# Two experts of each mixture in fixed places, and the loop of spare blocks moved behind the static blocks

## The reference

```python
pg = softmax(xt @ w_group + b_group)                    # 4 groups, the best one is taken
g_prob, g_idx = lax.top_k(pg, 1)
le = (xt @ w_expert + b_expert).reshape(N, 4, 8)[arange(N), g_idx[:, 0]]
e_prob, e_local = lax.top_k(softmax(le), 2)             # 2 of the 8 experts of that group
...
def expert_block(args):
    xb, e = args                                        # up to 128 rows of one expert
    return (silu(xb @ w_gate[e]) * (xb @ w_up[e])) @ w_down[e]
```

## Time and profile before

| | |
|---|---|
| median of 3 runs | 3689.51 us (3687.7 to 3690.94) |
| the profiled execution, its own time | 3681.5 us |
| its span in the trace | 3679.7 us |
| PE busy | 3420.4 us, 93% |
| DVE, ACT, POOL busy | 1617.9, 818.3, 364.8 us |
| m0 | 676 to 1233 us of the span |
| m1 | 1991 to 2548 us |
| m2 | 3300 to 3627 us |
| read from HBM | 752.52 MB, 227 GB/s over the span |

### The profile page before, as it was taken

The page is one execution under the profiler, slowest core; times in us unless marked ns, Lnnn a source line. Parts: engine busy times, 40 slices in busy tenths (PEclk is TensorE's granted clock), DMA queues, the critical chain, the costliest instruction groups (busy, mean ns, idle before and its releaser), DMA issues. The chain is left out here.

```text
span 3679.7 us, 51768 instructions
## 1 busy us (share of the span) xinstructions
PE 3420.4 (93%) x20970; PEld 1738.1 (47%) x20970; DVE 1617.9 (44%) x2560; ACT 818.3 (22%) x1822; POOL 364.8 (10%) x355
## 2 busy tenths in 40 slices
PE   9999999899999899999998998998899978997996
PEld 4444665433333344777754333333455658553332
DVE  4750886510111475777756111113341875462114
ACT  0000650100000122555511000000233551111112
POOL 0010300210000000000000200000000820003110
PEclk9999999899999999999999999999999999999998
DMA  9990211599999621000023999997421402219996
GB/s 373 361 336 0 93 70 69 227 416 427 423 424 424 251 91 57 26 1 1 1 92 142 403 425 425 426 421 303 149 82 68 149 18 79 101 66 371 419 418 267
DMA packets 146694, 818.42 MB, mean 222 GB/s; under 512 B 29875, under 2 KB 35635, under 8 KB 100374
## 3 DMA queue, kind: packets, MB, share of 16 engines
q1 hardware_dynamic: 117910, 737.21, 50.1%
q0 software_dynamic: 25808, 68.88, 4.9%
q10 hardware_dynamic: 2736, 8.95, 0.6%
HBM read 752.52 MB, written 82.55 MB: 227 GB/s over the span
## 5 line engine op out<-in xcount | busy, mean ns | idle before, releaser
L2320 PE MATMUL m_yp<-m_w,m_hidT 128*32 128x512 f32 (+2 forms) x2248 | 378.9, 596 | 10.5 <-issue 4.6
L2297 PE MATMUL m_up<-m_w,m_xT 128*32 128x512 f32 (+2 forms) x1792 | 305.4, 608 | 20.3 <-DMA m_w<-in_moe_w_up 20.3
L2297 PE MATMUL m_gp<-m_w,m_xT 128*32 128x512 f32 (+2 forms) x1792 | 300.7, 598 | 9.8 <-DMA m_w<-in_moe_w_gate 5.4
L2078 DVE TENSOR_TENSOR m_hid<-m_sg,m_up 128x512 f32<-128x512 f32 x42 | 28.9, 688 | 573.9 <-PE m_up L2297 573.9
L2073 DVE TENSOR_TENSOR m_yt<-m_yp,keep_flat 128x512 f32<-128x512 f32 x128 | 82.5, 686 | 398.7 <-PE m_yp L2320 388.9
L2320 PEld LDWEIGHTS m_yp<-m_w,m_hidT 128*32 128x32 f32 (+2 forms) x2248 | 121.7, 124 | 219.6 <-issue 214.1
L2378 ACT ACTIVATE m_sg<-m_gp 128x512 f32<-128x512 f32 (+1 forms) x64 | 33.5, 524 | 786.1 <-PE m_gp L2297 539.2
L2297 PEld LDWEIGHTS m_up<-m_w,m_xT 128*32 128x32 f32 (+2 forms) x1792 | 104.2, 126 | 216.0 <-issue 216.0
L2297 PEld LDWEIGHTS m_gp<-m_w,m_xT 128*32 128x32 f32 (+2 forms) x1792 | 97.5, 124 | 206.7 <-issue 204.1
L434 PE MATMUL front_acc<-front_hT,front_wt 128*128 128x512 f32 x448 | 194.4, 594 | 0.4 <-DVE q0T L535 0.4
L1233 PE MATMUL n_acc<-n_wt,n_hT 128*128 128x512 f32 (+2 forms) x512 | 190.5, 528 | 2.0 <-DMA n_wt<-in_w_in 1.3
(11 more groups left out here) (505 smaller groups left out, 5032.8 us busy)
## 6 DMA issues: line engine op xcount, KB each, us to landing
m_w<-in_moe_w_gate SPq DMA_DIRECT2D x64, 2048.0 KB
m_w<-in_moe_w_up SPq DMA_DIRECT2D x64, 2048.0 KB
m_w<-in_moe_w_down SPq DMA_DIRECT2D x64, 2048.0 KB
v<-in_ada_w SPq DMA_DIRECT2D x40, 1024.0 KB
m_w<-in_moe_w_gate SPq DMA_DIRECT2D x32, 1024.0 KB
m_w<-in_moe_w_up SPq DMA_DIRECT2D x32, 1024.0 KB
m_w<-in_moe_w_down SPq DMA_DIRECT2D x32, 1024.0 KB, 30.2
v<-in_w_mod SPq DMA_DIRECT2D x24, 1024.0 KB
```

The lines of the kernel that those rows point to most:

```text
L2297: last = pe.matmul(acc[part, 0:F], xT[:, j, k, part], w[:, place_of[m_, r][0], k * F:(k + 1) * F], start=k == 0, stop=k == KC - 1)
L2320: last = pe.matmul(yp[e][part, :], hidT[:, k, part], w[:, place_of["d", r][0], k * D + e * 512:k * D + (e + 1) * 512], start=k == 0, stop= ...
```

## The change: what it does, and the diff

Experts 21 and 22 (`PINS`) of every mixture always get ranks 28 and 29, whatever their number of rows, by a term of 2^17 or 2^18 in their sort key; the others are sorted among themselves. Their two blocks stand first. What is known of them ahead of the plan is used: SP issues their six matrices right behind the constants, without waiting for `plan`; DVE, PE and POOL make their row lists first (`number_pins`, `place_pin`, `list_pin`) and gather their rows. In `Layout` the order of loads is now gate, up of both pinned blocks, then down of both, then as before. `down(0)` and `down(1)` stay where they were in PE's order, behind `gate_up(1)` and `gate_up(2)`. The loop of spare blocks goes behind the main part on all engines, with 8 turns for 7, and with waits so that it starts when the main part's slots and stores are done. `place_rows` goes behind the first `copy_x` on DVE, and on POOL the token numbers are stored behind the fourth gather (the fifth in m2).

```diff
-        self.spill = 21
+        self.spill = 24
+        self.pinned = [r for _, parts in large[0:2] for r, _, _ in parts]
-        self.blocks = (large[0:1] + pair[0:1] + lone[0:3] + pair[1:3] + large[3:4] + second + pair[3:4] + lone[3:6] + pair[4:5] + large[1:2] + pair[5:6]
+        self.blocks = (large[0:2] + pair[0:1] + lone[0:3] + pair[1:3] + large[3:4] + second + pair[3:4] + lone[3:6] + pair[4:6]
...
-        turns = [(m, i) for n in range(self.N + 1) for m, i in order(n) if 0 <= i < self.N]
+        pinned = range(len(self.pinned))
+        turns = [(m, i) for i in pinned for m in up] + [(m, i) for i in pinned for m in down]
+        for n in range(len(self.pinned), self.N + 1):
+            turns += [(m, n) for m in up if n < self.N] + [(m, n - 1) for m in down if n - 1 not in pinned]
+        self.early = 3 * len(self.pinned)
...
+                def number_pins():
+                    for k in range(2):
+                        step(dve.tensor_tensor(pin_of[k][:, :, :], hot[k][:, :, place_in:place_in + PINNED],
+                                               shift[:, k].unsqueeze(2).to_broadcast([P, T, PINNED]), ALU.mult))
+                    step(dve.tensor_tensor(pin_of[0][:, :, :], pin_of[0][:, :, :], pin_of[1][:, :, :], ALU.add))
+                    step(dve.tensor_tensor(pin_of[0][:, :, :], pin_of[0][:, :, :], og[:, :, group_of:group_of + 1].to_broadcast([P, T, PINNED]), ALU.mult))
+                def place_pin(i):
+                    if i == 0:
+                        dve.wait_ge(rank_cp, 1)
+                        dve.wait_ge(a_in, 48)
+                    step(dve.tensor_tensor(xT[:, i], across[:, :].unsqueeze(1).to_broadcast([P, T, P]),
+                                           rank[:, :, PINS[i]].unsqueeze(2).to_broadcast([P, T, P]), ALU.is_equal), f"pin{i}")
+                def list_pin(i):
+                    column = slice(i, i + 1)
+                    dve.wait_ge(pin_done[i], 1)
+                    step(dve.tensor_scalar(pin_row[:, column], pin_ps[i][:, 256:257], float(UNUSED_ROW), None, ALU.add))
+                    step(dve.tensor_scalar(pin_second[:, column], pin_row[:, column], float(S), float(S), ALU.is_ge, ALU.mult))
+                    step(dve.tensor_tensor(pin_ri[:, column], pin_row[:, column], pin_second[:, column], ALU.subtract), f"pin_rows{i}")
+                    step(dve.tensor_copy(pin_goal[:, column], pin_row[:, column]), f"pin_goals{i}")
...
                 choose()
+                number_pins()
                 rank_experts()
+                for i in range(PINNED):
+                    place_pin(i)
+                list_pin(0)
                 list_rows()
                 count_spills()
+                turn_lists()
+                copy_x(dve, dve.tensor_copy, 0, 0)
                 place_rows()
+                copy_x(dve, dve.tensor_copy, 1, 0)
+                product(0)
+                weigh_rows()
...
             def _(sp):
                 for dst, src in zip((tri, ones, across), constants):
                     sp.dma_start(dst[:, :], src).then_inc(a_in, 16)
+                for m_, r, slot, _ in layout.units[:EARLY]:
+                    sp.dma_start(w[:, slot], sources[m_][layer * X + PINS[layout.pinned.index(r)]]).then_inc(w_in[slot], 16)
                 sp.wait_ge(e_set, 1)
...
-                for unit in layout.units[:AHEAD]:
+                for unit in layout.units[EARLY:]:
                     load(*unit)
...
             def _(pool):
+                for n in range(PINNED):
+                    pool.wait_ge(d, at[f"pin_rows{n}"])
+                    gather(n)
                 pool.wait_ge(d, at["rows"])
-                for n in range(DEEP):
+                for n in range(PINNED, DEEP):
                     gather(n)
+                gather(DEEP)
...
+                def list_pin(i):
+                    pe.wait_ge(d, at[f"pin{i}"])
+                    for t in range(T):
+                        last = pe.matmul(pin_ps[i][:, 256:257], xT[:, i, t], pin_of[0][:, t, i:i + 1], start=t == 0, stop=t == T - 1)
+                    last.then_inc(pin_done[i], 1)
...
                 plan()
-                keep_clock(pe, turn[0], ident, 5)
+                list_pin(0)
+                rank_tables()
+                for i in range(1, PINNED):
+                    list_pin(i)
+                keep_clock(pe, turn[0], ident, 3)
                 list_rows()
+                turn_x(0)
+                gate_up(0)
+                turn_x(1)
+                for n in range(1, N):
+                    gate_up(n)
+                    turn_hid(n - 1)
+                    if n + 1 < N:
+                        turn_x(n + 1)
+                    down(n - 1)
+                turn_hid(N - 1)
+                down(N - 1)
                 pe.sem_inc(so_dn, 1)
                 spills = spilled(pe)
...
-                keep_clock(pe, turn[0], ident, 4)
```

More of the change, by code:

```diff
@@ L1788 @@
 HALF_P = P // 2
+PINS = 21, 22
 class Layout:
@@ L1854, in mixture @@
     ROWS = N + SPILL_BLOCKS
-    AHEAD = 2 * RING // 3
-    taken = {slot for _, _, slot, _ in layout.units[:AHEAD]}
-    spare = [s for s in range(RING) if s not in taken][:3]
+    spare, EARLY = range(3), layout.early
+    PINNED = len(layout.pinned)
+    group_of, place_in = PINS[0] // PER_GROUP, PINS[0] % PER_GROUP
+    assert [p // PER_GROUP for p in PINS] == [group_of] * PINNED and [p - PINS[0] for p in PINS] == list(range(PINNED))
     BASE = N * P
@@ L1991, in rank_experts @@
                     dve.wait_ge(counted, 1)
[L1992 to L1993 removed]
+                    step(dve.scalar_tensor_tensor(key[:, :], cnt_ps[:, 0:X], float(X), keyed, ALU.mult, ALU.add))
+                    step(dve.scalar_tensor_tensor(own_key[:, :], cnt_ps[0:X, X:X + 1], float(X), own_keyed[0:X, :], ALU.mult, ALU.add))
@@ L2139, in _ @@
                 held(sp, st.marks, so_st, spills * (16 * GROUP) + 16)
[L2140 to L2145, removed]
-                sp.wait_ge(ahead_in, 16 * len(ahead))
                 for j in range(2):
@@ L2151, in _, with column @@
             def _(pool):
+                def column(n, general, pinned):
+                    b = layout.blocks[n][0]
+                    return pinned[:, n:n + 1] if n < PINNED else general[:, b:b + 1]
                 def gather(n):
@@ L2196, in _ @@
                             i = turn_no * GROUP + j
+                            for e in range(2):
+                                pool.wait_ge(stored[e], 16 * ((N + 1 - e) // 2))
                             pool.wait_ge(so_dn, i + 1)
@@ L2396, in _ @@
                 act.sem_inc(so_st, 16)
+                copy_x(act, act_copy, 0, 1)
+                act.wait_ge(d, at["owners"])
+                silu(0)
+                copy_x(act, act_copy, 1, 1)
+                for n in range(1, N):
+                    silu(n)
+                    copy_hid(n - 1)
+                    if n + 1 < N:
+                        copy_x(act, act_copy, n + 1, 1)
+                copy_hid(N - 1)
                 spills = spilled(act)
@@ L3144, in host_constants @@
     moe += [part[:, None] + P * np.arange(TILES)[None, :] - UNUSED_ROW + k * S for k in range(2)]
+    above = np.array([2.0 ** (17 + PINS.index(e)) if e in PINS else 0.0 for e in range(N_EXPERTS)])
+    free = N_EXPERTS - len(PINS)
+    pinned = Layout(0, 18).pinned
+    others = iter(range(free))
+    ranks = [free + pinned.index(r) if r in pinned else next(others) for r in range(N_EXPERTS)]
+    moe += [np.pad(above + np.arange(N_EXPERTS), (0, P - N_EXPERTS))[:, None], np.tile(above + np.arange(N_EXPERTS), (P, 1)), np.tile(ranks, (P, 1))]
     moe = np.concatenate(moe, axis=1)
```

119 lines of the change are left out of this document (56 added, 63 removed).

## The result

| | before | after |
|---|---|---|
| median of 20 runs each | 3688.95 us (3684.53 to 3698.45) | 3696.24 us (3687.21 to 3703.13) |
| ratio after to before | | 1.0015, 95% interval 1.0010 to 1.0021 |
| the profiled execution, its own time | 3681.5 us | 3688.1 us |
| its span in the trace | 3679.7 us | 3686.3 us |

The kernel became slower by 0.15%, some 5.5 us, where 11.5 us less was forecast. (The two medians as listed lie 7.3 us apart; the ratio, to which the interval belongs, is the figure used here.) The two profiled executions differ by 6.6 us, so they show the same thing and can be compared stretch by stretch. I count each stage from the moment at which the stage before it has cleared its semaphores.

What follows compares the result with a forecast made beforehand. The prediction took m0 and m1 as bound by weight transfers, m2 narrowly so at its end. Terms m0 -1.2, m1 -1.3, m2 -10.5, loops +1.5 gave -11.5 us: 3670.0 profiled, 3678.0 from the median, range 3661 to 3697.

Steps and rivals of the forecast that it cites:

- The start of the loads: Start of each mixture: first load at about 677.3 instead of 688.35 in m0, 11.0 us earlier, m1 and m2 too.
- The start of PE: Start of m0: first gate matmul in effect at 707.1 against 715.25, with 1.7 us added twice for the clock.
- third rival: Start of the mixtures: clock halved, 12 us in place of 3.4, in all +7.7 us, 3697; chance 0.13.
- Where the gain stalls: m0 and m1: load 14 waits for `down(1)`, DMA engines idle 10 us, load 36 only 1.2 and 1.3 us earlier.
- No stall: m2, ring of 18 slots: no load is held up by a slot; gain taken as 10.5 us.
- The loop at the end: End of each mixture: POOL's loop runs beside its closing drain, costing 0.5 us per mixture, 1.5 in all.
- second rival: End of each mixture: POOL's drain starts only behind the loop, 18.3 us in all, 3695 to 3713; chance 0.15.
- first rival: Load 14 doesn't hold the queue back; each mixture ends 11 us earlier, -31.5 us in all, 3658; chance 0.17.
- the signs that I named: Expected: DMA dip near 765 and 2080. Wrong if no dip, or last store to next stage over 8 us.

Runs made afterwards that it cites:

- e1: The changed kernel without the loop of spare blocks on all five engines; ratio to the kernel before 0.9996.
- e5: The changed kernel with one branch around the loop of spare blocks and ring slots given in PE's order; ratio to the kernel before 0.9925.
- e12: e5 with token-number stores and reading back in m0 and m1 only where spare blocks exist; ratio to the kernel before 0.9903.
- e8: The changed kernel with its first six loads held back until the plan; ratio to the kernel before 1.0085.
- e7: The kernel before with one branch around its loop of spare blocks, at its old place; ratio to the kernel before 0.9994.
- e3: The changed kernel with the ring's slots given in the order in which PE frees them; ratio to the kernel before 0.9958.
- e2: The changed kernel without the loop of spare blocks on POOL alone; run once, no ratio, last store to next stage 7.0, 7.0, 7.2 us.

## Why the prediction was wrong

**The start of the loads: right.** 11.0 us were forecast, 11.0 and 10.6 came in m0 and m1. In m2 it was 9.4 in the profiled run, since one of SP's issues took 2.04 us, and 11.0 in e1.

**The start of PE: 2 us too early, by a halved clock in another place.** In m0 I had `gate_up(0)` 31.5 us behind the start of the stage (707.1); it came at 33.5. I priced the 16 short matmuls of `list_pin` at 1.87 us by the earlier trace rows, and they took 3.37 and 3.57. Their first three weight loads stand 0.11 us apart, as in the earlier trace rows, the others 0.21, and between them, at 686.7, TensorE's granted clock falls to half, until 700.4. DVE waited 2.3 and 3.1 us for them, not 0.75, so the step `numbered` ended 3.6 us late. The windows (PEclk is the third number from the end), first in the kernel before, then after the change:

```profile
686.00:690.00 4.00, 3.94 (x13) 1.99 (x14) 3.76 (x8) 0.19 (x1) 0.00 (x0) 1.00 0.27 53
```

```profile
686.00:690.00 4.00, 3.53 (x17) 3.51 (x18) 1.69 (x3) 0.00 (x0) 0.00 (x0) 0.59 1.00 426
690.00:694.00 4.00, 4.00 (x20) 3.94 (x20) 1.61 (x7) 0.25 (x1) 1.12 (x1) 0.50 1.01 430
...
706.00:710.00 4.00, 3.27 (x9) 1.56 (x8) 3.62 (x12) 0.60 (x1) 2.05 (x2) 0.65 1.00 420
```

PE was busy 2.8 of the 6 us ahead of 686, and 4.1 in the same stretch of the kernel before. In this place the kernel before runs ten `keep_clock` matmuls (4.56 us from 686.27), which the change takes out, and its clock stays full until 698.4; that their absence lets the clock fall is argued, not tried. The table, for which I had added 1.7, ran at full clock but for its first 0.2 us and lost 0.1. A second fall, from 707.2 to 710.6, cost 1.7 in the first gate matmuls of m0 (8.80 us instead of 7.1), as I had it, and the same in m2, but nothing in m1 (7.10). So the third rival had the right mechanism in the wrong place, and 12 us was too much for it: with all this PE began 2 us late, and `down(1)` ended some 1 us late.

**Where the gain stalls: the mechanism right, its price low.** Load 14 was issued at 770.2, when `down(1)` ended, and the DMA engines lay idle as forecast. But load 36 landed 226.1 us behind the start, against 222.2 by my sum and 223.2 before. Three pieces: load 14 issued 0.9 us later counted from the start of the stage, 0.6 more until it had landed, and the pace. I took 5.43 us per load from loads 36 to 70 and used it for loads 14 to 36, where both traces have 5.54 in m0; 22 loads make 2.4 us. In the changed kernel nearly all of it lies in loads 15 and 16, 6.6 us each, which land while POOL reads back the spare rows (99.5 to 114 us behind the start); from load 16 on the 5.43 holds. I had priced that reading at 0. It needn't be all of it, since these two are also the first behind the gap; but in e5, without a gap, loads 17 and 18 took 6.3 us each in that stretch, and 5.5 in e12, without the reading. The kernel before has the slower pace too, although its reading back was over at 78 us, before load 14; why isn't known. Worked backwards from load 36 with the same number, my sum also put load 14 of the kernel before 2.6 us too late. So m0 and m1 were not 1.2 and 1.3 us faster but 2.3 and 1.8 slower up to PE's end.

**m2: 10.5 forecast, 6.3 measured.** The step "No stall" was right in that no gap of the transfers shows; but load 14 landed 13.5 us earlier than before and load 36 only 5.8. In between the loads went 3.50 us apart instead of 3.16, while SP had them issued 12.8 us and more ahead of their landing, so it was the transfers and no missing slot. The token stores and the reading back now lie in this stretch. The traces speak for them: in the kernel before, where the stores lay beside loads 6 to 13, it was these that went 3.70 us apart (2.86 after the change), and in e8, with the loads later against the same stores, again loads 6 to 13 (3.74) and not 14 to 36 (3.11). That they are the whole cause isn't shown: m2 needs them, and no run took them away there. Besides, `place_rows`, which I costed at nothing because of 14 us of PE's work, held back the copy for block 1: in m2 block 0 takes PE only 8.8 us, and PE stood idle 1.5 us ahead of block 1. e7 showed that such idle time of PE isn't what sets m2's end.

**The loop at the end: the step that failed.** "I take it beside, 0.5 per mixture, since the drain is a wait for work that is under way." The drain didn't behave as such a wait. It took 4.9 us from where POOL reached it (5.05 in m2), whether the store's issue had just ended or the store was 4 us old, and the loop stood ahead of it: 3.2, 3.0 and 4.5 us, 10.7 in all instead of 1.5. Of the 4.4 us of the loop in m0 only 3.2 counted, because POOL's sequencer ran the first part of it while the last store was still being issued, which the end had to wait for in any case. Both ends were in the range I had worked out (0 and 5.6); I chose the wrong one, although the distance of 7 us behind the last store, against 3 for the store itself, spoke for a fixed cost. This is the mechanism of the second rival, at a little over half of the 18.3 us that I gave it; it had a chance of 0.15. None of the three ends had a branch of 6 us: POOL's 24 branches of the loop took 50 to 60 ns. The fetch of code that the Trainium skill describes ("Runtime: NRT & Kernel Launch", Instruction fetch mechanics) doesn't show on POOL there. PE's first branch took 3.4 to 4.2 us, but it ended 0.2, 0.3 and 1.7 us behind PE's last matmul, so it may have waited for the matmuls; which it was stays open, and it didn't set the end.

**The sum.** Forecast -11.5; the loop +9.2, m0 and m1 +6.6 against their terms, m2 +4.2, the other stages -1.9: +6.6, as measured. The first rival, that the head start stays, is what e3 made true by hand. The measured median of 3696.24 lies just inside the range that I gave, 3661 to 3697, and next to the third rival's 3697, but by luck: the upper end was that rival's, and the time came from the loop. Of the signs that I named, the dip near 765 and 2080 appeared as forecast (759 to 771, 2082 to 2090), and so did the distance of over 8 us from the last store to the next stage, which I had named as one that would prove me wrong.

## What to carry to other kernels

A load that starts earlier is worth what the slowest link behind it passes on: find the first load that waits for a slot, ask which instruction frees it in the engine's real order, and compare that time with the landing of the load before it. An order of slots worked out by a list has to be the order in which the engine frees them. And work moved behind the last store is free only on engines that have nothing fixed to do after it; an empty loop of eight turns cost nothing on DVE, and 3 to 4.5 us on POOL, where one branch around it took that away. Besides, look at the granted clock of the row from which a price is taken and of the place where it is used: the short matmuls cost 1.87 us at full clock and 3.4 at half of it.

## What the runs showed of the hardware that was not expected

- POOL's closing drain, in stages that stored by indirect DMA, took 4.88 to 5.05 us in the changed kernel's mixtures, even when 4 us had passed since the store. In e2, reached right behind the start of the store, it lasted 5.26 to 5.63. In m0 and m1 of e12, which left out 16 indirect stores and a reading back, it ended 0.8 us sooner.
- 16 matmuls with a single column and 128x128 weights took 3.4 us, with weight loads 0.21 us apart, at a granted clock of 0.50; 16 with 36 columns took 1.87 us, 0.11 apart, as did the first three of the single-column ones, before the clock fell.
- The 16 stores of 128 token numbers and one reading back cost the loads beside them about 3 us up to the last load at 530. Beside and just behind them the DMA engines were as busy as ever, but moved 292 GB/s instead of 423 (e5 and e12).
